# A mixture-of-experts decoder layer: one expert's down load made to wait for the row gathers, and 80 small matrix products moved from behind the first expert to behind the twenty-ninth

## The reference

```python
def hier_moe(h, ...):
    # group by argmax of 4 logits, then the top 2 of the 8 experts in the group
    expert = grp[:, None] * EXPERTS_PER_GROUP + top_idx       # 2 of 32 experts for each token
    # tokens sorted by expert, in blocks of rows of one expert
    def block(args):
        toks, wts, e = args
        xb = h_pad[toks]                                       # gather of the rows
        a = xb @ w_exp_gate[e]                                 # 1024 x 512
        u = xb @ w_exp_up[e]                                   # 1024 x 512
        return ((jax.nn.silu(a) * u) @ w_exp_down[e]) * wts    # 512 x 1024
    y = segment_sum(y_rows, row_tok)                           # two rows for each token
```

## Time and profile before

| | us |
|---|---|
| runs | 1460.38, 1449.18, 1461.34; median 1460.38 |
| the profiled execution | 1463.75, of which the span from its first to its last instruction is 1461.9 |
| PE busy | 1316.7 (90%) |
| matmuls' idle time ahead of the large group, put down to the up weights | 55.5 |
| 372.65 MB moved, mean | 255 GB/s |

### The profile page before, as it was taken

How to read it: one execution, slowest core, us unless ns; L and a number is a source line. 1 busy time by engine, 2 the same in 40 slices (tenths; PEclk the granted TensorE clock), 3 DMA queues, 4 the chain that set the end, 5 groups by cost and what they waited for, 6 DMA issues and landing times.

```text
span 1461.9 us, 19698 instructions
## 1 busy us (share of the span) xinstructions
PE 1316.7 (90%) x7561; PEld 764.4 (52%) x7561; DVE 334.0 (23%) x822; ACT 283.6 (19%) x600; POOL 208.8 (14%) x298
## 2 busy tenths in 40 slices
PE   4899999899999999999999999699788788787786
PEld 2334787344667686778888845443333233222232
DVE  2333020654333414220000023711101101101104
ACT  3100567332323233210000022200000000000002
POOL 1214333321011102020000010101100101100000
PEclk9999999987999999999999999699999999999998
DMA  9958999967725243332310542689999999999974
GB/s 356 381 220 200 335 362 314 323 230 231 234 58 152 70 126 101 80 87 65 94 58 0 220 171 51 216 338 377 421 427 422 425 425 423 424 424 421 425 319 187
DMA packets 115472, 372.65 MB, mean 255 GB/s; under 512 B 10932, under 2 KB 56389, under 8 KB 95934
## 3 DMA queue, kind: packets, MB, share of 16 engines
q1 hardware_dynamic: 93664, 308.96, 55.4%
q0 software_dynamic: 19936, 57.72, 12.1%
q10 hardware_dynamic: 1790, 4.87, 1.2%
HBM read 359.22 MB, written 22.36 MB: 261 GB/s over the span
## 4 chain that ended last, share of the span: by engine, by line
PE 71%; DMA 22%; DVE 4%; ACT 2%; issue 1%; SPq 0%; POOL 0%; POOLq 0%; ACTq 0%; DVEq 0%
PE ps L1546 64%; DMA ring<-in_w_exp_up 19%; PE ps L1557 7%; DMA ring<-in_w_ada 1%; DMA work<-in_x_prompt 1%; DVE work L1243 1%; DMA work<-h_rows,idx 1%; DVE work L1535 0%; SPq L442 0%; DVE work L1540 0%; ACT hx L681 0%; DMA work<-expert_rows 0%; DVE work L1508 0%; ACT work L712 0%; DMA expert_rows<-work 0%
## 5 line engine op out<-in xcount | busy, mean ns | idle before, releaser
L1546 PE MATMUL ps<-ring,work 128*64 128x512 f32 (+3 forms) x2880 | 475.9, 499 | 76.6 <-DMA ring<-in_w_exp_up 55.5
L1546 PEld LDWEIGHTS ps<-ring,work 128*64 128x64 f32 (+2 forms) x2880 | 175.3, 131 | 336.4 <-issue 262.3
L1546 PE MATMUL ps<-ring,hx 128*128 128x256 f32 (+3 forms) x880 | 222.4, 446 | 2.3 <-DMA ring<-in_w_in 2.3
L1546 PE MATMUL ps<-hx,ring 128*128 128x272 f32 x768 | 179.1, 393 | 0.6 <-DVE work L1243 0.6
L1546 PEld LDWEIGHTS ps<-ring,hx 128*128 128x128 f32 (+1 forms) x880 | 136.6, 175 | 79.5 <-issue 64.4
L1546 PEld LDWEIGHTS ps<-hx,ring 128*128 128x128 f32 x768 | 145.2, 190 | 31.2 <-DVE work L1243 1.1
L1546 PE MATMUL ps<-work 32*128 32x256 f32 (+12 forms) x914 | 115.0, 357 | 13.6 <-DVE work L998 5.8
L1546 PE MATMUL ps<-work,ring 128*128 128x272 f32 (+2 forms) x464 | 97.7, 369 | 0.7 <-ACT ring L888 0.7
L926 ACT ACTIVATE work<-ps 128x256 f32<-128x256 f32 x32 | 12.3, 384 | 436.6 <-PE ps L1546 436.6
L1557 PE MATMUL ps<-cst,ring 128*128 128x128 f32 x632 | 89.7, 285 | 7.2 <-DVE ring L1162 2.7
L1546 PEld LDWEIGHTS ps<-work,ring 128*128 128x128 f32 (+1 forms) x464 | 81.4, 188 | 18.6 <-issue 2.7
(11 more groups left out here) (291 smaller groups left out, 786.0 us busy)
## 6 DMA issues: line engine op xcount, KB each, us to landing
ring<-in_w_exp_down SPq DMA_DIRECT2D x32, 2048.0 KB, 22.4
ring<-in_w_exp_gate SPq DMA_DIRECT2D x31, 2048.0 KB, 18.2
ring<-in_w_exp_up SPq DMA_DIRECT2D x31, 2048.0 KB, 22.7
ring<-in_w_ada SPq DMA_DIRECT2D x12, 2048.0 KB, 19.0
ring<-in_cache_k SPq DMA_DIRECT2D x64, 256.0 KB, 4.9
ring<-in_cache_k POOLq DMA_DIRECT2D x64, 256.0 KB, 5.5
ring<-in_cache_v SPq DMA_DIRECT2D x64, 256.0 KB, 4.7
ring<-in_cache_v POOLq DMA_DIRECT2D x64, 256.0 KB, 5.0
```

Source lines behind the costliest of these rows:

```text
L1546: return pe.matmul(out, lhsT, rhs, start=start, stop=stop, **k)
```

## The change

It adds a wait on SP ahead of the down load of expert 1: both first gathers must have landed. It moves `further_places` on PE from behind `gate_up(0)` to behind `down(28)`, and on DVE the wait for it with the six instructions that follow to between the steps of experts 28 and 29; for that, DVE's loop is one round shorter and its last round is written out. `rows_to` uses another free place for its intermediate, since by then the old one holds results of experts.

```diff
@@ SP
             sp.wait_ge(s("h2_out1"), 16 * 2)
+            for p in range(2):
+                sp.wait_ge(s(f"xs_in{p}"), 16)
             down_load(5, expert_row(1))
             gate_up_blocks(3, 0, 1)
@@ DVE
             def rows_to(at, n, bank, src):
-                to = run.rearrange("p a e -> p (a e)")[:, 0:n]
+                to = work[:, 10624:10624 + n]
...
-            dve.wait_ge(*after("more_ps"))
-            dve.tensor_scalar(idx[:, NE // 2:], ps[:, 5, 0:MORE // 2], -1.0, None, ALU.add)
-            rows_to(NE, MORE, 5, MORE // 2).then_inc(*done("more_ready"))
...
             for e in range(4):
                 dve_step(e, 0, e % 2, e, True)
-            with dve.Fori(1, NE // 4) as i:
+            with dve.Fori(1, NE // 4 - 1) as i:
                 for r in range(4):
                     dve_step(4 * i + r, i, r % 2, r)
+            dve_step(NE - 4, NE // 4 - 1, 0, 0)
+            dve.wait_ge(*after("more_ps"))
+            dve.tensor_scalar(idx[:, NE // 2:], ps[:, 5, 0:MORE // 2], -1.0, None, ALU.add)
+            rows_to(NE, MORE, 5, MORE // 2).then_inc(*done("more_ready"))
+            for e in range(NE - 3, NE):
+                dve_step(e, NE // 4 - 1, e % 2, e % 4)
@@ PE
             for e in range(4):
                 gate_up(e, e // 2 * 2 + 2, e // 2, 1 if e == 3 else 0, e % 2, weight_pair(e))
-                if e == 0:
-                    further_places()
                 rows_turned((e // 2 + 1) // 2, (e // 2 + 1) % 2, e % 2)
                 down(e, e // 2, e % 2, 3 * (e % 2) + 2)
...
                 down(e, e // 2, e % 2, 3 * (e % 2) + 2)
+                if e == NE - 4:
+                    further_places()
```

## The result

The changed kernel takes 1453.12 us (median of 20 runs, 1440.94 to 1456.46), the one before 1461.26 (20 runs): ratio 0.9949, 95% interval 0.9926 to 0.9972, 8.1 us less. The forecast was 7.8 less. The profiled execution took 1453.05, its span 1451.3. Of all runs in this document three, of 1684.15, 4520.04 and 4754.93 us, fell in a much slower state and are left out of every median.

What follows compares the result with a forecast made beforehand. Experts bound by their bytes, so the end depends on when transfers stop pausing, set by PE between the indices and expert 3. 3.1 + 3.6 + 1.1 = 7.8 us off 1460.38 gives 1452.6 us, range 1443 to 1460.

Steps and rivals of the forecast that it cites:

- Part 1, the gather: Ahead of expert 1's down load: first gather alone lands in 3.9 us, not 8.1; gate_up(0) starts 4.2 us sooner, bounds 0 to 4.6.
- The clock in gate_up(0): In gate_up(0): if the half-speed clock rises no sooner, 1.9 of 4.2 us are kept; middle taken, 3.1.
- Rival 4: Clock stays low over gate_up(0), down(0) and gate_up(1): 14.6 us of slow pairs, 1467.2 us; chance 0.03.
- Part 2, early place: Between gate_up(0) and down(0): without the 80 products the pause falls from 5.7 to 2.1 us, gain 3.6.
- the fall of the clock: Behind the small products, in down(0) and gate_up(1): the fall costs 1.3 us; 1.1 taken as gain, bounds 0 and 1.3.
- Can the transfers follow?: From expert 3's weights to the full stream: transfers can give at most 10.4 us, so all 7.8 arrive.
- the bound of 10.4: Most the stream can gain up to 1002: 3.1 us of earlier start plus 7.3 of lacking rate.
- the sum: PE reaches down(1) and every later early release 3.1 + 3.6 + 1.1 = 7.8 us sooner.
- Part 2, late place: Behind down(28): gate_up(29) starts 1.1 to 3.9 us later, free up to a 9 us delay, then one for one.
- the sign that was named: At the end of the experts: the last up load lands about 21 us minus its delay after its issue.

Runs made afterwards that it cites:

- wait_only: The kernel before plus only SP's wait for both first gathers ahead of expert 1's down load; 1457.61 us, ratio 0.9977 to the kernel before.
- the second set: The unchanged kernel before and the changed kernel measured again, beside the experiments; 1461.30 and 1444.38 us, ratio 0.9900.
- late_plus3: The changed kernel with the 80 products behind down(28) done three times more, results unused; 1458.3 us, ratio 1.0007 to the kernel before.
- move_only: The changed kernel without SP's wait for the two gathers; 1457.78 us, ratio 0.9968 to the kernel before.
- behind_down0: The changed kernel with the 80 products behind down(0) and DVE's part behind expert 0's step; 1456.23 us, ratio 0.9970 to the kernel before.
- first_only: The changed kernel with SP waiting for the first gather alone ahead of the down load; 1451.41 us in its one run.

## Why the prediction was right

**Part 1, the gather.** Taken as 3.9 us alone, measured 3.6: gate_up(0) starts 4.6 us sooner, forecast 4.2, bound 4.6. What I drew from the Trainium skill's rule of taking turns (DMA: Bandwidth & Descriptors, Queues, rings and completion order), that a load ahead would cost a small gather well under 1 us, the runs refute: 2 MB cost 4.0 to 4.5 us. They don't show whether the rule or my use of it is at fault.

**The clock in gate_up(0).** I took off 1.1 us. It took 9.22 us against 8.88, so only 0.3 went; the other profiles with nothing ahead of the gather show 9.02 to 9.64. The rise kept its distance from the first large products rather than its place: from 943.5 to 947 the clock of the changed kernel stood at 0.93. This term was 0.8 too pessimistic. Rival 4, a low level over three groups of products, is out: behind 950.6 the clock stood at 1.00.

**Part 2, early place.** 3.6 us of pause were forecast, and 5.7 against 2.1 were measured, which is the same. Of the fall of the clock I counted 1.1 of the 1.3 us; it is gone in full, and back in `wait_only`. PE is 9.2 us sooner by expert 5's weights, forecast 7.8.

**Can the transfers follow?** Yes: 8.8 us at gate_up(31), below the bound of 10.4, and the rate before the full stream rose. The median moved by 8.1.

**How much of it is luck.** The mechanisms are those that the sum names, but the sum is 1.4 us short of PE's 9.2: 0.4 at the gather, 0.8 and 0.2 at the two terms of the clock. That the forecast still met the median so closely, 7.8 against 8.1, is in part luck: in the second set the same two kernels lie 16.9 us apart, because the groups of runs fell otherwise.

**Part 2, late place.** The price was right and its reason wrong. I wrote that the queue covers a late release up to 9 us. For the loads that may hold; but PE's own work behind the products, three experts of 12.6 us each, is the shorter cover, since it holds only the waits of 2.33, 0.89 and 2.58 us, 5.8 in all: two in the earlier trace rows, the last in this row of the timeline before.

```profile
1418.10 8.78 PE L1546 MATMUL ps<-ring,work 128*64 128x512 f32 x32 [2.58 <-DMA ring<-in_w_exp_up]
```

The products take some 3.4 of these; 1.3 and 4.5 were found left in the two profiles, and in `late_plus3` none, at a cost. The sum came out right all the same, but a place that is more than half full was called 9 us deep. The last up load landed 18.8 us after its issue instead of 21.2, the sign that was named.

**Ahead of the gather.** Not foreseen: in both profiles of the changed kernel the first gather is released by the landing of the last rows, 0.5 to 0.6 us behind what the indices would allow. The change isn't the reason, since `move_only`, without the wait, shows the same 0.5, and `behind_down0` and `first_only`, with a wait, don't. A gather faster still would bring little: PE now waits only 1.43 us for it, behind its own products of the places.

## What to carry to other kernels

In a stage bound by its bytes, look for the last moment at which the transfers pause. What delays the engine that frees the buffers ahead of that moment costs in full (here behind gate_up(0) as behind down(0)), and behind it is free as long as that engine still waits. How long it is free is the sum of that engine's own waits up to the end, not the depth of the queue. A small transfer on the critical path should be issued with nothing large ahead of it that isn't needed at once.

## What the runs showed of the hardware that was not expected

The runs of each kernel fall in two groups, most clearly in the first set: of 20 before, 7 have a median of 1451.3 and 13 of 1462.3; of 20 after, 4 have 1443.0 and 16 have 1453.2. Which group is hit more moves the median of a kernel by several us (before: 1461.30 in one set, 1454.89 in another), more than a part of this change. Like with like, the change is worth 8.3 and 9.1 us. The profiles show where they part. Windows from 324 to 355 us, of the kernel before and of `wait_only` (1445.41 us in its profiled execution):

```profile
324.00:355.00 31.00, 29.42 (x147) 13.10 (x146) 13.06 (x42) 7.58 (x24) 6.44 (x12) 0.72 0.48 161
```

```profile
324.00:355.00 31.00, 31.00 (x197) 15.08 (x197) 17.05 (x55) 10.86 (x32) 6.44 (x12) 1.00 0.96 311
```

In the first PE's granted clock is 0.72 and 147 matmuls are done, in the second it is 1.00 and 197. Over 300 to 400 us the clock was 1.00 in three profiles, whose first gather is issued at 920 to 922, and 0.83 to 0.88 in the other ten, at 929 to 937. Whether the clock or something ahead of it comes first there was not tried.

The clock fell under a busy PE: in `late_plus3` the 320 small products began at a granted clock of 1.00 and went on at 0.52, while the record has PE busy without a break (the windows above). The Trainium skill (TensorE: Matmul & The Clock Gate, What's actually happening) says that how busy PE has been of late sets the clock. As far as the profile's busy time can say, these rows don't bear that out: PE was busy 11.60 of 11.60 us at 0.52.
